# A weight ring's lower halves at four different start addresses modulo 256 bytes

## What is computed

```python
h = rms_norm(x, g_mix)
... = jnp.split(h @ w_in, offs, axis=-1)
...
x = x + jnp.concatenate([oa, ob, oc, od], axis=-1) @ w_out
x = x + jnp.square(jax.nn.relu(rms_norm(x, g_mlp) @ w_up)) @ w_down
x = x + (ple.astype(x.dtype) @ w_ple) * jax.nn.sigmoid(rms_norm(x, g_ple) @ w_ple_gate)
```

## The kernel before

| tensor | begins at | modulo 256 | step |
|---|---|---|---|
| `hhi` (moving) | 36992 | 128 | 1280 per block |
| `xhi` (moving) | 92288 | 128 | 1280 per block |
| `xlo` (moving) | 112832 | 192 | 1280 per block |
| `hlo` (moving) | 182336 | 64 | 1280 per block |
| `hlast`, `pleh`, `plel` (moving) | 216736, 221856, 224416 | 160 | 1280 per block |
| `ring` | 136064 | 128 | 4096 per slot |
| `whi` (weights) | 152448 | 128 | 4096 per slot |
| `wlo` (weights) | 75904 | 128 | 4096 per slot |

## Time and profile before

### The profile page before, as it was taken

The page is one execution under the profiler, slowest core; times in us unless marked ns, Lnnn a source line. Parts: engine busy times, 40 slices in busy tenths (PEclk is TensorE's granted clock), DMA queues, the critical chain, the costliest instruction groups (busy, mean ns, idle before and its releaser), DMA issues.

```text
span 3378.1 us, 60314 instructions
## 1 busy us (share of the span) xinstructions
PE 3285.3 (97%) x20664; PEld 2977.2 (88%) x20664; DVE 1229.2 (36%) x2211; ACT 1138.0 (34%) x1666; POOL 2223.1 (66%) x2989
## 2 busy tenths in 40 slices
PE   7999999999999999999989999999999999999998
PEld 5777766799999999999977776668999999999998
DVE  4334564542041230323253445545411402304143
ACT  3333332433333333334343432424333333333342
POOL 4655200388898898888765551005888988889885
PEclk9999999999999999999999999999999999999999
DMA  5443322354454554544453433224545445455443
GB/s 153 134 123 111 111 73 83 100 152 152 151 151 155 150 152 154 150 154 151 133 157 114 129 93 112 71 84 124 149 151 155 150 151 155 150 152 154 150 145 123
DMA packets 295722, 453.02 MB, mean 134 GB/s; under 512 B 36336, under 2 KB 111344, under 8 KB 294832
## 3 DMA queue, kind: packets, MB, share of 16 engines
q1 hardware_dynamic: 295328, 448.66, 44.0%
q0 software_dynamic: 144, 0.87, 0.1%
HBM read 435.54 MB, written 14.06 MB: 133 GB/s over the span
## 4 chain that ended last, share of the span: by engine, by line
PE 91%; DVE 3%; issue 2%; DMA 1%; ACT 1%; SPq 1%; POOL 0%; DVEq 0%; ACTq 0%; POOLq 0%
PE ps L707 21%; PE ps L708 21%; PE ps L706 20%; PE ps L804 5%; PE ps L792 5%; PE ps L767 5%; PE ps L770 4%; PE ps L769 3%; PE ps L896 2%; DMA ring<-in_w_in 1%; PE ps L931 1%; PE ps L842 1%; PE ps L900 1%; PE ps L899 1%; PE ps L865 1%
## 5 line engine op out<-in xcount | busy, mean ns | idle before, releaser
L669 POOL TENSOR_TENSOR wlo<-ring,whi 128x256 fp32r<-128x256 f32 x2400 | 1803.5, 785 | 786.5 <-ACT whi L1141 786.0
L1141 ACT ACTIVATE whi<-ring 128x1024 fp32r<-128x1024 f32 x600 | 635.9, 1061 | 1350.3 <-PE ps L708 1341.6
L707 PE MATMUL ps<-xlo,whi 128*128 128x320 f32 x2560 | 794.9, 311 | 0.0
L708 PE MATMUL ps<-xhi,whi 128*128 128x320 f32 x2560 | 788.0, 308 | 0.0
L706 PE MATMUL ps<-xhi,wlo 128*128 128x320 f32 x2560 | 781.7, 305 | 0.0
L708 PE MATMUL ps<-hhi,whi 128*128 128x320 f32 x2176 | 672.2, 309 | 0.0
L706 PE MATMUL ps<-hhi,wlo 128*128 128x320 f32 x2176 | 659.3, 303 | 0.0
L655 POOL TENSOR_TENSOR rlo<-ring,whi 128x256 fp32r<-128x256 f32 (+2 forms) x576 | 415.9, 755 | 325.4 <-ACT whi L1125 325.4
L707 PE MATMUL ps<-hlo,whi 128*128 128x320 f32 x2048 | 629.9, 308 | 0.0
L706 PEld LDWEIGHTS ps<-xhi,wlo 128*128 128x128 f32 x2560 | 483.8, 189 | 0.6
L708 PEld LDWEIGHTS ps<-xhi,whi 128*128 128x128 f32 x2560 | 480.6, 188 | 0.0
(11 more groups left out here) (244 smaller groups left out, 3160.7 us busy)
## 6 DMA issues: line engine op xcount, KB each, us to landing
ring<-in_w_up SPq DMA_DIRECT2D x256, 512.0 KB, 3.7
ring<-in_w_down SPq DMA_DIRECT2D x256, 512.0 KB, 3.6
ring<-in_w_in SPq DMA_DIRECT2D x120, 512.0 KB, 3.6
ring<-in_w_out SPq DMA_DIRECT2D x64, 512.0 KB, 4.0
ring<-in_w_ple_gate SPq DMA_DIRECT2D x64, 512.0 KB, 3.6
xsave<-x SPq DMA_DIRECT2D x8, 640.0 KB, 5.9
x<-xsave SPq DMA_DIRECT2D x8, 640.0 KB, 4.3
ring<-in_w_in SPq DMA_DIRECT2D x16, 288.0 KB, 2.9
```

Source lines behind the costliest of these rows:

```text
L669: last = nc.gpsimd.tensor_tensor(wlo[:, s, c:c + LO_COLS], ring[:, s, c:c + LO_COLS], whi[:, s, c:c + LO_COLS].bitcast(f32), ALU.subtract)
L707: mm(out, hi[:, k, cols], xl, start=False, stop=False)
L708: return mm(out, hi[:, k, cols], xh, start=False, stop=stop)
L1141: A(whi[:, s, :], ring[:, s, :], ACT.Copy).then_inc(hi_ready, 1)
```

## The change

`wlo` gets slots of 1040 instead of 1024 columns, and begins 192 bytes earlier. Of each slot the first 1024 columns are used, as before; the slice in `tail_unit` says so for `whi` and `wlo` alike (for `whi` it changes nothing). The slots begin at 75712, 79872, 84032 and 88192, that is at 192, 0, 64 and 128 modulo 256 bytes, where before all four began at 128. The last slot keeps both its address and its remainder; the last used byte is where it was.

```diff
-        wlo = sb("wlo", [128, RING, 1024], f32r, top[0] - 4 * RING * 1024)
+        wlo = sb("wlo", [128, RING, 1024 + 16], f32r, top[0] - 4 * RING * (1024 + 16) + 64)
...
             def tail_unit(l, q4, u):
 
                 hold(lo_ready, l * HL + N_WU + 4 * q4 + u + 1 - TAIL0)
-                return [w[:, u % RING, :].rearrange("p (a n) -> p a n", a=UK) for w in (whi, wlo)]
+                return [w[:, u % RING, 0:1024].rearrange("p (a n) -> p a n", a=UK) for w in (whi, wlo)]
```

## The result

The changed kernel takes **3400.32 us** at the median of four runs (3398.97 to 3401.74), against 3378.28 us for the kernel before in the same comparison: 22 us, or 0.65%. Over all the runs, in which one of the kernel before at 3391.3 us counts too, the ratio is 1.0048, with a 95% interval of 1.0029 to 1.0068. It is slower, clear of the noise: on the edge of the 0.5% that the prediction called no change, outside the forecast's own range of 3365 to 3390 us, and inside the whole range.

The account below looks back on a forecast made before the run. The prediction took PE's matmul rate in the two tails as the bound. Its terms for POOL, for SP, ACT and DVE, and for PE's weight loads were 0 + 0 + 0, giving a median of 3378 us, range 3352 to 3406.

Parts of the forecast that it names:

- The bound: In the two tails, 62% of the span, only PE's rate from one matmul to the next sets the time.
- POOL, ACT, SP, DVE at 0: POOL's writes of wlo keep their time, hidden in any case; the other three touch no moved bytes: 0 us.
- Rival 3: In the tails, POOL's pieces exceed 867 ns and POOL becomes the bound: up to 315 us more, 3693 us; chance 0.03.
- The term of PE's weight loads at 0: Tail matmuls loading wlo from moved slots keep their summed pace: 0 us, between -18 and +26.
- Rival 2: In the tails, changing weight addresses lose the faster 144.4 ns rhythm for 147.4: 26 us more, 3404 us; chance 0.23.
- Rival 4: Part of the slower 147.4 ns tail stretches joins the faster rhythm: 7 us saved, 3371 us; shares the forecast's 0.48.
- Rival 1: At L708, wlo loads stop colliding with the moving stream: 18 us saved, 3360 us; sign: twelve chunks at most 328; chance 0.26.
- The rule of the Trainium skill: For PE's weight loads: two independent read ports, so no address can matter and time stays exactly as before.

Follow-up runs that it names:

- E4: Changed kernel, its wlo addresses kept, with PE loading the whi half where it loaded wlo: 3382.21 us, ratio 0.9999 to the kernel before.
- E8: Kernel before with xlo and hlo, the lower halves of the activations, stepped 64 bytes per pair of blocks, weights unmoved: 3395.23 us, ratio 1.0034.
- E1: Kernel before with all four wlo slots at 192 modulo 256, 4096 bytes apart: 3399.22 us, ratio 1.0056.
- E3: Kernel before with all four wlo slots at 64 modulo 256, 4096 bytes apart: 3412.29 us, ratio 1.0095.
- E2: Kernel before with all four wlo slots at 0 modulo 256, 4096 bytes apart: 3411.2 us, ratio 1.0091.
- E6: Kernel before with both whi and wlo slots at 192, 0, 64 and 128 modulo 256: 3414.66 us, ratio 1.0095.
- E10: Kernel before with wlo slots 4128 bytes apart, at 32, 64, 96 and 128 modulo 256: 3406.74 us, run once.
- E5: Kernel before with every hand-placed tensor 64 bytes higher: 3384.42 us against 3384.18, ratio 0.9995.
- E9: Kernel before with xlo and hlo stepped 16 bytes per pair of blocks and hlo 96 bytes higher: 3405.73 us, run once.

## Why the prediction came out as it did

- **The bound.** That PE's pace sets the tail, and nothing else can move it, was right. All of the loss but 1 us is in the distance between matmuls, at a granted clock of 1.00.
- **POOL, ACT, SP, DVE at 0.** Right: POOL's pieces went from 742 to 740 ns at the median, and E4 shows PE undisturbed by POOL's writes at the new addresses. Rival 3 had no ground.
- **The term of PE's weight loads at 0: this step failed.** It was sized from the moving operand ("a shift by 64 bytes either way costs the same, and that the sum stays"). The rows behind it had `hlo` and `xlo` at two different places with the same 433.3 ns, and that is true; but the two places are both good ones. E8 shows the others: 440 ns where the lower half has the upper half's remainder. For the weight address, E1 to E3 show 437 to 442 ns, and up to 447, at all three new remainders. The place of before was the best one tried. The term measured +21 us in the tails' profile, where the forecast had 0, between -18 and +26.
- **Rival 2 had the sign and the price, not the mechanism.** It put +26 us on a fast rhythm broken by the alternation. The runs without alternation cost +14 (E1), +29 (E2) and +23 us (E3) in the tails, so a constant address costs as well, and alternation is not needed. The mean of these and 0 for the unmoved slot is 16.6 us, where the changed kernel lost 21. In the up product the mean fits (437.9 ns a product from both); in the down product it gives 436.9 or 439.1 ns, depending on which of E3's two paces is used, against 440.2 measured. So a few us may come from the change of slot after all, in the down product: slot 2 takes the slower of E3's two paces, and slot 3 needs four products to come back to 433. That the time lies inside the range is owed to this rival's price, which was worked out for a mechanism that the runs do not need: in this the range was lucky. Its ceiling of 147.4 ns per matmul was too low, too: slot 2 in the down product runs at 447 / 3 = 149. What was right in it is that a rhythm persists and can be missed: it shows in E3's two groups, and in slot 3 of E6 and E10.
- **Rival 4 came true in part.** The chunks that ran at 147.4 ns in the kernel before run at 146.0. That is 2 x 6 x 192 = 2,304 matmuls by 1.4 ns, 3 us back. With it the account of the tails nearly closes: in each layer 14 chunks of the up product and the gate by 1.6 ns a matmul (4.3 us), 16 of the down product by 2.3 (7.1 us), less 1.6 us, makes 9.8, or 19.6 us for both layers, of the 21 measured; 1.0 us more is the time without work in the second tail.
- **Rival 1 fell.** No address brought a product below 433.3 ns for long. A collision beside L708 alone, of loads and streams at the same remainder, would have given a gain in at least one of the three places. Its sign was set too low besides: at the 5.0 ns of its price the 576 moved matmuls of the twelve chunks save 2.9 us and leave 329.9, not 328. The formula behind its 3347 us is given in the Trainium skill, "TensorE: Matmul & The Clock Gate", section "Back-to-back issue gap", for a matmul taken by itself and set apart from a stream of weight loads and matmuls, which is what runs here. No chunk of any run came under 144.4 ns a matmul.
- **The rule of the Trainium skill**, "SBUF — State Buffer", section "Who interferes with whom", that TensorE has two independent read ports and never waits on anyone, carried part of the forecast of no change. The measurement decides against what the prediction drew from it, that no address can matter: E1 to E3 move nothing but the weight address (and with it POOL's write, which E4 clears) and cost 0.56 to 0.95%. Whether PE's two reads wait for each other is not shown by that.

## What to carry to other kernels

Where matmuls with new weights follow one another without a gap, the start addresses of weights and moving operands relative to each other can matter: here, with 128 x 128 weights and 320 columns in float32r, they were worth up to 3% of the pace (433 to 447 ns a product). Other shapes were not tried. No row of waits shows it: count matmuls over a stretch. Treat placement as something to be measured by slot, since a ring with four different places tries four in one run; but let each candidate also run alone, because a unit can inherit a pace from the one before. Equal paces at two places are no evidence about a third.

## What was not expected of the hardware

- The pace of equal matmuls locks into one of several values: 144.4, 145.6, 145.9, 146.1, 146.7, 147.4 and 148.9 ns were seen over whole chunks with constant remainders. Two of them occur on identical addresses (144.4 and 147.4 in the earlier trace rows, 145.9 and 148.9 in E3).
- An interruption can switch the pace. In the first up product and in the gate, and nowhere else in the MLP products and the gate, other matmuls (L750) stand between the first and the second chunk. In the gate of the kernel before:

```profile
1610.42 0.31 PE L708 MATMUL ps<-xhi,whi 128*128 128x320 f32 x1
1610.57 0.70 PE L750 MATMUL ps<-acc,ones 128*128 128x320 f32 x2
1610.87 0.55 PE L706 MATMUL ps<-xhi,wlo 128*128 128x320 f32 x1
```

  There the kernel before goes from 433.3 to 442 ns a product and stays until the chunks end. In E4 (both layers) and in E5 (layer 0) the first up product went on at 433.3 ns behind the same matmuls; why is open.
- Steps of 16 bytes in a moving operand's address change the pace of a unit (3.46 to 3.53 us within 64 bytes, E9, run once).
- A common shift of everything by 64 bytes changes nothing (E5, ratio 0.9995).

What in the memory or in PE makes these rhythms was not settled: no run here separates the two reads in time, and none removes the weight loads.
